# Two-block transformer kernel: the odd mixer's query/key units as 512-column products over two PSUM banks, and their move to the VectorE evacuation

## The chip, the cores and the metric

The kernel runs on one core of one Trainium2 chip. The metric is the device time of one execution in microseconds (us); before the change the median of three runs is 980.25 us (979.71 to 980.5).

## The reference, cut to what matters

Two transformer blocks run over 256 tokens of width 1024. The change lies in the second layer of the first block, the odd mixer (an mLSTM):

```python
p = (h @ w_in).astype(jnp.float32)          # h: 256 x 1024 (rmsnorm of x)
qk, v, og, ig_pre, fg_pre = jnp.split(p, splits, axis=-1)
qk = causal_conv_silu(qk, conv_w, conv_b)   # 4 taps along the tokens, 1024 channels
q, k = jnp.split(qk, 2, axis=-1)
...
ig = soft_cap(ig_pre + gb[0])               # 4 heads each
lf = jax.nn.log_sigmoid(soft_cap(fg_pre + gb[1]))
out = mlstm_scan(q, k, v, lf, ig)
```

## The kernel before, in words

**Products in two parts.** Every float32 weight w and activation h is split into a high and a low part (wh + wl, hh + hl). A projection is the sum of three products in the fp32r type: wh with hh, wh with hl, wl with hh. ScalarE (ACT) makes wh from the loaded weights (`high`, L1763), VectorE (DVE) makes wl by a subtraction (`split`, L1168: a helper for every tensor_tensor), both some three units ahead (AHEAD = 3) in rings of four slots (RING = 4).

**Units.** The weights are a list of 1 MB units (UNITS), taken in order by every engine's own loop `for u in range(NU)`. A unit of the kind F has 1024 rows by 256 columns: TensorE (PE) takes it as two groups g of 128 columns, each with 8 slabs k. A unit of the kind T has 512 rows by 512 columns, and two of them make one result. The order around the change is mv 0, mv 1, mqk 0 to 3, mv 2, mv 3, mog 0 to 3, then out2. The four mqk units are the query and key columns. hx holds hh and hl side by side, 256 tokens each.

**Two ways to do a unit of kind F.** `f_forward` puts both groups into one PSUM bank (2 x 256 columns) and issues, for each g and k, three products of 256 columns. `f_wide`, used for the units named in WIDE (attention and convolution of the second block), gives each group a bank of its own: 8 products of wh with the 512 columns of hh and hl together, then 8 products of wl with hh's 256 columns (`both_parts`). It needs a sum at the end: ACT copies columns 256 to 511 of each bank to the unit's home in SBUF (L2072) and counts S["wide"]; DVE then adds columns 0 to 255 to it (L1168, `tt(wide_home(u, g), wide_bank(u, g)[:, 0:SEQ], ...)`), twice a unit.

**The mqk units before.** They go through `f_forward`. ACT copies the bank of 2 x 256 columns to m_raw, a part of the arena (L2084). Between the products of mqk 0 lie 16 small products for the gates (`gate_product`, one after each slab's three).

**What DVE does there, in the order of its loop.** In the iteration of mqk 1: the gate sums gz (wait for PE's gmm), gz again after ACT's tanh (S["gcap"]), `split` of the unit three further on, and `conv_taps` of mqk 0 (one product with the row of rms values, then eight tap instructions). In the iteration of mqk 2: split, `conv_taps` of mqk 1. In mqk 3: gg and gB (from PE's gate_cumsum, counted S["g"]), split, `conv_taps` of mqk 2. In mv 2: a copy and a scan for the running maximum (S["M"], L1545, L1546), split, `conv_taps` of mqk 3. In mv 3: gm, eight instructions for m_w (S["warg"]), then `ml_probs` 0 and 1 (S["ms"]). All of this is one in-order queue.

**What PE does there.** After mqk 2: gate_cumsum; after mqk 3: gate_rows (wait for S["g"]); then mv 2; ml_scores 0 and 1; mv 3 with gate_max 0 and 1 among its first products (wait for S["M"]); ml_scores 2, which waits for `ml_probs(0)` because it takes the same bank (`eng.wait_ge(S["ms"], h - 1)`), and for S["qk"] at 4, ACT's silu of the last query/key pair; then mog 0.

Of the kernel before, what the change touches and what calls it, by code (L numbers as in the profile page):

```python
# [27 lines left out]
KT = D // P  # L28
# [126 lines left out]
def mlp(us, layer):  # L155
    for j in range(9):
# [12 lines left out]
NU = len(UNITS)  # L169
SLABS = {"F": KT, "C": KT, "T": 4, "B": 2}  # L170
EVAC = {"hf": "act", "hq": "act", "hi": "act", "rq": "dve", "rk": "dve", "rv": "act", "hgate": "act",
        "rgate": "act", "uw0": "act", "uw1": "act", "up0": "dve", "up1": "dve", "mqk": "act", "mv": "act", "mog": "act",
        "aq": "dve", "ak": "dve", "av": "act", "ag": "dve", "cc": "dve", "cx": "dve", "cb": "dve",
        "cg": "dve", "mc": "act", "ma": "act"}

# [4 lines left out]
_count, _in_bank, _next = {"act": 0, "dve": 0}, [None, None], 0  # L180


WIDE = ("aq", "ak", "ag", "cc", "cx", "cb", "cg")
WIDE_OF, PAIR_OF = {}, {}
for _u, (_kind, _, _, _, _role, _i) in enumerate(UNITS):
    if _role in WIDE:
        _n = WIDE_OF[_u] = len(WIDE_OF)
        PAIR_OF[_u] = ((3, 5), (2, 4), (0, 1))[_n % 3] if _n < 8 else ((3, 5), (0, 1))[_n % 2]
        if PAIR_OF[_u] == (0, 1):
            for _t in range(2):  # L190
                BEFORE[_u, _t] = _in_bank[_t]
                _in_bank[_t] = (_u, None)
        _count["dve"] += 1
        EVAC_AT[_u, None] = _count["dve"]
    elif _kind == "F":
        BANK_OF[_u] = _next
        BEFORE[_u, _next] = _in_bank[_next]
        _in_bank[_next] = (_u, None)
        _next ^= 1
        _count[EVAC[_role]] += 1  # L200
        EVAC_AT[_u, None] = _count[EVAC[_role]]
    elif _kind == "T":
        assert _next == 0
        T_OF[_u] = len(T_OF) // 2
        for _t in range(2):
            if _i % 2 == 0:
                BEFORE[_u, _t] = _in_bank[_t]
                _in_bank[_t] = (_u + 1, _t)
            else:
                _count[EVAC[_role]] += 1  # L210
                EVAC_AT[_u, _t] = _count[EVAC[_role]]
# [51 lines left out]
def build(nc, a, out):  # L263
    ctx = ExitStack()
    with ctx:
# [113 lines left out]
        m_raw = view(4096, 4, 2, SEQ)  # L379
# [183 lines left out]

        def wide_home(u, g):
            role, i = UNITS[u][4:]
            if role in ("aq", "ak", "ag"):
                return {"aq": a_q, "ak": a_k, "ag": a_g}[role][:, 2 * i + g, :]
            return (c_u if role == "cc" else c_t)[:, g * SEQ:(g + 1) * SEQ]
# [73 lines left out]
        def _(eng):  # L642
# [67 lines left out]
            def both_parts(o, u, g):  # L710

                c = slice(g * P, (g + 1) * P)
                for k in range(KT):
                    mm(o[:, :], slot(wh, u)[:, k, c], hx[:, k, :, :].rearrange("p a t -> p (a t)"), k == 0, False)
                for k in range(KT):
                    m = mm(o[:, 0:SEQ], slot(wl, u)[:, k, c], hh[:, k, :], False, k == KT - 1)
                return m

            def f_wide(u):

                n, w_hi, w_lo = WIDE_OF[u], slot(wh, u), slot(wl, u)
                if PAIR_OF[u] == (0, 1):
                    for t in range(TT):
                        wait_bank(eng, u, t)
                else:
                    for v in [v for v in WIDE_OF if v < u and PAIR_OF[v] == PAIR_OF[u]][-1:]:
                        wait_evac(eng, v)
                if u not in LOW_LAST:
                    for g in range(2):
                        m = both_parts(wide_bank(u, g), u, g)  # L730
                else:
                    for g in range(2):
                        for k in range(KT):
                            mm(wide_bank(u, g)[:, :], w_hi[:, k, g * P:(g + 1) * P], hx[:, k, :, :].rearrange("p a t -> p (a t)"), k == 0, False)
                    wait_low(eng, u)
                    for g in range(2):
                        for k in range(KT):
                            m = mm(wide_bank(u, g)[:, 0:SEQ], w_lo[:, k, g * P:(g + 1) * P], hh[:, k, :], False, k == KT - 1)
                m.then_inc(S["used"], 1)
# [16 lines left out]
            def f_forward(u):  # L756
                w_hi, w_lo, o = slot(wh, u), slot(wl, u), bank(u)
                wait_bank(eng, u, BANK_OF[u])
                for g in range(2):
                    for k in range(KT):  # L760
                        c, dst = slice(g * P, (g + 1) * P), o[:, g * SEQ:(g + 1) * SEQ]
                        mm(dst, w_hi[:, k, c], hh[:, k, :], k == 0, False)
                        mm(dst, w_hi[:, k, c], hl[:, k, :], False, False)
                        m = mm(dst, w_lo[:, k, c], hh[:, k, :], False, k == KT - 1)
                        if (g, k) == (1, KT - 1):
                            m.then_inc(S["used"], 1)
                        if u == at("mqk"):
                            gate_product(KT * g + k)

            def t_forward(u):  # L770

# [224 lines left out]
            def gate_max(j):  # L996

                if j == 0:
                    eng.wait_ge(S["M"], 1)
                for h in (2 * j, 2 * j + 1):  # L1000
                    mm(PS[5 + j][:, (h % 2) * SEQ:(h % 2 + 1) * SEQ],
                       ident[0:HEADS, h:h + 1].broadcast_to([HEADS, P]), MT, True, True)
                if j == 1:
                    for tt in range(TT):
                        m = eng.transpose(PS[7][:, 256 + 4 * tt:260 + 4 * tt], MT[:, tt * P:(tt + 1) * P],
                                          ident[0:HEADS, 0:HEADS])
                    m.then_inc(S["Mb"], 1)

            def ml_scores(h):
                eng.wait_ge(S["qk"], 2 if h < 2 else 4)  # L1010
                if h >= 2:
                    eng.wait_ge(S["ms"], h - 1)
                q, k, o = m_qk[:, h, :], m_qk[:, HEADS + h, :], PS[2 + h % 2]
                mm(o[:, 0:SEQ], k[:, 0:P], q, True, True)
                mm(o[:, SEQ:SEQ + P], k[:, P:2 * P], q[:, P:2 * P], True, True).then_inc(S["msc"], 1)
# [740 lines left out]
        def _(eng):  # L1756
# [246 lines left out]
            for u in range(-AHEAD, NU):  # L2003
# [42 lines left out]
                elif role in ("uw0", "uw1") and u in SECOND:  # L2046
                    for t in range(TT):
                        wait_evac(eng, u, t)
                        act(wf[:, half_of(t)], wf[:, half_of(t)], ACT.Square).then_inc(S["sq"], 1)
                elif UNITS[u][0] == "T" and i % 2 == 1 and u not in SECOND:  # L2050
                    for t in range(TT):
                        t_evac(u, t)
                elif role in ("rq", "rk"):
                    wait_used(eng, u)
                    j, swapped = rope_at(u)
                    if j >= 2:
                        eng.wait_ge(S["rope"], j - 1)
                    half = P // 2
                    for lo, hi in ((0, half), (half, 0)):
                        eng.copy(swapped[lo:lo + half], pair[hi:hi + half]).then_inc(S["swap"], 1)  # L2060
                elif role in WIDE:
                    if role == "cc" and i >= 1:
                        eng.wait_ge(S["c_gated"], i)
                    elif role == "cx":
                        eng.wait_ge(S["y_src"], i)
                    elif role == "cb":
                        eng.wait_ge(S["c_prod"], i + 1)
                    elif role == "cg":
                        eng.wait_ge(S["c_gated"], i + 1)
                    wait_used(eng, u)  # L2070
                    for g in range(2):
                        m = eng.copy(wide_home(u, g), wide_bank(u, g)[:, SEQ:2 * SEQ])  # L2072
                    m.then_inc(S["wide"], 1)
                elif role in ("up0", "up1"):
                    layer = 0 if role == "up0" else 1
                    c = slice(512 * (i % RING), 512 * (i % RING + 1))
                    wait_evac(eng, u)
                    act(wf[:, c], wf[:, c], ACT.Square).then_inc(S["sq"], 1)
                    eng.wait_ge(S["sq"], 16 * layer + i + 1)
                    if i >= RING:  # L2080
                        wait_used(eng, at(f"out{2 * layer + 1}", i - RING))
                    eng.copy(flat2(yh, i % RING), wf[:, c]).then_inc(S["yh"], 1)
                elif role == "mqk":
                    eng.copy(m_raw[:, i, :, :], pair).then_inc(S["evac_act"], 1)  # L2084

                if u == at("hf", 1):
                    eng.wait_ge(S["f"], 1)
# [77 lines left out]
```

## Time and profile before

| what | value |
|---|---|
| median of 3 runs | 980.25 us (979.71 to 980.5) |
| the profiled execution: time / span | 979.72 / 977.9 us |
| PE busy | 968.2 us, 99% |
| PE weight loads busy | 854.6 us, 87% |
| DVE busy | 661.6 us, 68% |
| ACT busy | 522.4 us, 53% |
| the mqk units on PE | 382.69 to 409.99 us |

Busy time of an engine is a mean over the span; a matmul's record is longer than the distance to the next one, since they are pipelined, so PE's pace is read from start to start.

### The profile page before, as it was taken

How to read it: one execution, taken by the hardware profiler on the slowest of the kernel's cores; microseconds unless marked ns; L12 is line 12 of the kernel's file. 1: busy time of each engine (PE TensorE's matmuls, PEld its weight loads, DVE VectorE, ACT ScalarE, POOL GpSimd, SP SyncE). 2: the span in 40 equal slices, each digit the busy share in tenths (PEclk: the TensorE clock that was granted, in tenths of full speed). 3: DMA queues.
4: the chain of work that ended last, by engine and by line, in shares of the span. 5: the costliest groups of instructions: out<-in, count | busy, mean ns of one | idle time of the engine just before them, and what ended most of it. 6: DMA issues, size and time to landing. Idle time of an engine off the chain costs nothing.

```text
span 977.9 us, 13743 instructions
## 1 busy us (share of the span) xinstructions
PE 968.2 (99%) x5616; PEld 854.6 (87%) x5616; DVE 661.6 (68%) x859; ACT 522.4 (53%) x671; POOL 13.9 (1%) x12
## 2 busy tenths in 40 slices
PE   9999999999999999999999999999999999999997
PEld 8898888899999988978899999987888888888885
DVE  6889646676666658766676666668655788756463
ACT  7744464654444447655664444448445576545533
POOL 0000000000000000000000000000000000002000
PEclk9999999999999999999999999999999999999999
DMA  9953526467777674534467777764865545566611
GB/s 328 300 173 129 172 92 196 137 213 250 243 237 226 227 238 133 186 129 129 151 215 225 260 229 232 247 183 145 271 205 178 170 134 170 172 213 222 210 44 44
DMA packets 122867, 187.32 MB, mean 192 GB/s; under 512 B 5332, under 2 KB 88757, under 8 KB 122805
## 3 DMA queue, kind: packets, MB, share of 16 engines
q1 hardware_dynamic: 122368, 186.05, 58.0%
q8 instruction: 45, 0.74, 0.3%
q10 hardware_dynamic: 436, 0.40, 0.1%
q14 instruction: 18, 0.14, 0.0%
HBM read 185.37 MB, written 1.06 MB: 191 GB/s over the span
## 4 chain that ended last, share of the span: by engine, by line
PE 93%; DVE 4%; ACT 1%; DMA 1%; issue 1%; DVEq 0%; ACTq 0%
PE bank L644 91%; DVE arena L1174 1%; DVE wl L1168 1%; DMA raw<-in_ev_w_in 1%; PE bank L878 1%; ACT wh L1763 1%; PE bank L968 0%; DVE arena L1171 0%; ACT arena L1758 0%; DVE arena L1168 0%; PE bank L1049 0%; ACT L1758 0%; PE bank L838 0%; PE bank L707 0%; DVE hx L1174 0%
## 5 line engine op out<-in xcount | busy, mean ns | idle before, releaser
L1168 DVE TENSOR_TENSOR wl<-raw,wh 128x2048 fp32r<-128x2048 f32 (+1 forms) x157 | 356.8, 2275 | 174.5 <-ACT wh L1763 101.1
L1763 ACT CAST wh<-raw 128x2048 fp32r<-128x2048 f32 x155 | 294.7, 1910 | 138.5 <-PE bank L644 134.8
L644 PE MATMUL bank<-hx,wh 128*128 128x256 f32 (+1 forms) x1728 | 346.1, 314 | 0.1
L644 PEld LDWEIGHTS bank<-hx,wh 128*128 128x128 f32 x1728 | 278.5, 191 | 15.9 <-issue 0.7
L644 PE MATMUL bank<-hx,wl 128*128 128x256 f32 x1088 | 238.6, 283 | 0.0
L644 PEld LDWEIGHTS bank<-hx,wl 128*128 128x128 f32 x1088 | 181.6, 191 | 4.4
L644 PE MATMUL bank<-wh,hx 128*128 128x512 f32 x576 | 184.4, 393 | 0.8 <-ACT arena L1758 0.5
L644 PE MATMUL bank<-wh,yh 128*128 128x512 f32 x416 | 162.7, 391 | 0.0
L644 PE MATMUL bank<-wl,yh 128*128 128x512 f32 x416 | 162.0, 390 | 0.0
L644 PE MATMUL bank<-wh,yl 128*128 128x512 f32 x416 | 161.9, 389 | 0.0
L644 PEld LDWEIGHTS bank<-wh,hx 128*128 128x128 f32 x576 | 107.9, 188 | 24.0 <-issue 1.9
L644 PE MATMUL bank<-wl,hx 128*128 128x512 f32 x288 | 112.2, 390 | 0.0
L644 PEld LDWEIGHTS bank<-wh,yl 128*128 128x128 f32 x416 | 78.1, 188 | 16.4
L644 PEld LDWEIGHTS bank<-wh,yh 128*128 128x128 f32 x416 | 78.2, 188 | 15.5
L644 PEld LDWEIGHTS bank<-wl,yh 128*128 128x128 f32 x416 | 78.2, 188 | 15.5
L1758 ACT ACTIVATE work<-work 128x512 f32<-128x512 f32 x32 | 20.0, 631 | 99.7 <-DVE work L1174 99.7
L1168 DVE TENSOR_TENSOR arena<-bank,arena 128x256 f32<-128x256 f32 (+1 forms) x88 | 40.6, 492 | 44.4 <-ACT arena L2072 28.0
L644 PEld LDWEIGHTS bank<-wl,hx 128*128 128x128 f32 x288 | 54.1, 188 | 10.7
L2072 ACT COPY arena<-bank 128x256 f32<-128x256 f32 x56 | 18.1, 376 | 72.5 <-PE bank L644 72.5
L1758 ACT ACTIVATE arena<-bank 128x512 f32<-128x512 f32 (+2 forms) x58 | 28.4, 498 | 35.0 <-PE bank L644 34.9
L1174 DVE SCALAR_TENSOR_TENSOR arena<-raw,cf,arena 128x256 f32<-128x256 f32 x84 | 40.7, 485 | 3.0
L1758 ACT ACT_TABLE_LOAD x26 | 33.4, 1283 | 4.3 <-PE bank L644 2.0
(184 smaller groups left out, 627.0 us busy)
## 6 DMA issues: line engine op xcount, KB each, us to landing
raw<-in_mlp_w SPq DMA_DIRECT2D x64, 1024.0 KB, 5.6
raw<-in_w_in SPq DMA_DIRECT2D x40, 1024.0 KB, 5.1
raw<-in_ev_w_in SPq DMA_DIRECT2D x19, 1024.0 KB, 5.2
raw<-in_w_ada SPq DMA_DIRECT2D x12, 1024.0 KB, 5.2
raw<-in_od_w_in SPq DMA_DIRECT2D x12, 1024.0 KB, 5.5
raw<-in_ev_w_out SPq DMA_DIRECT2D x6, 1024.0 KB, 4.8
raw<-in_od_w_out SPq DMA_DIRECT2D x4, 1024.0 KB, 4.9
raw<-in_w_o_conv SPq DMA_DIRECT2D x4, 1024.0 KB, 4.9
```

Source lines behind the costliest of these rows:

```text
L644: return eng.matmul(o, l, r, start=start, stop=stop, skip_group_check=True)
L878: m = eng.transpose(x_half(t, k), src[:, t, k * P:(k + 1) * P], ident[:, :])
L1168: return eng.tensor_tensor(o, x, y, op)
L1174: return eng.scalar_tensor_tensor(out=o, in0=x, scalar=c, in1=y, op0=op0, op1=op1)
L1758: return eng.activation(o, x, f, **more)
L1763: eng.copy(part(wh, u), part(raw, u)).then_inc(S["hi"], 1)
L2072: m = eng.copy(wide_home(u, g), wide_bank(u, g)[:, SEQ:2 * SEQ])
```

## The change

The units mqk 0 to 3 join WIDE and so go through `f_wide`, in the bank pairs (6, 7), (0, 1), (2, 3), (5, 6). Of the three products a slab, wh with hh and wh with hl become one of 512 columns. The home is m_raw. ACT's one copy of 512 columns a unit becomes two of 256, and DVE gets two additions of 128 x 256 a unit, at the place in its loop where f-units are evacuated: behind `conv_taps` of the unit before. The evacuation counts on DVE's semaphore. The gate products of mqk 0 stand behind the products of wl. Three waits are added on PE: mqk 2 and 3 wait for the evacuation of mqk 0, gate_max for that of the last unit in bank 6, ml_scores 0 and 1 for that of mqk 2. The second block's units keep their bank pairs.

```diff
-        "rgate": "act", ..., "mqk": "act", "mv": "act", "mog": "act",
+        "rgate": "act", ..., "mqk": "dve", "mv": "act", "mog": "act",
...
-WIDE = ("aq", "ak", "ag", "cc", "cx", "cb", "cg")
+WIDE = ("mqk", "aq", "ak", "ag", "cc", "cx", "cb", "cg")
...
-        PAIR_OF[_u] = ((3, 5), (2, 4), (0, 1))[_n % 3] if _n < 8 else ((3, 5), (0, 1))[_n % 2]
+        if _n < 4:
+            PAIR_OF[_u] = ((6, 7), (0, 1), (2, 3), (5, 6))[_n]
+        else:
+            PAIR_OF[_u] = ((3, 5), (2, 4), (0, 1))[(_n - 4) % 3] if _n < 12 else ((3, 5), (0, 1))[_n % 2]
...
+            if role == "mqk":
+                return m_raw[:, i, g, :]
...   in both_parts
                 for k in range(KT):
                     m = mm(o[:, 0:SEQ], slot(wl, u)[:, k, c], hh[:, k, :], False, k == KT - 1)
+                    if u == at("mqk"):
+                        gate_product(KT * g + k)
...   in f_wide
+                elif n in (2, 3):
+                    wait_evac(eng, at("mqk"))
...   in f_forward
-                        if u == at("mqk"):
-                            gate_product(KT * g + k)
...   in gate_max
                 if j == 0:
                     eng.wait_ge(S["M"], 1)
+                    wait_wide(eng, 6)
...   in ml_scores
                 if h >= 2:
                     eng.wait_ge(S["ms"], h - 1)
+                else:
+                    wait_evac(eng, at("mqk", 2))
...   on ScalarE
-                elif role == "mqk":
-                    eng.copy(m_raw[:, i, :, :], pair).then_inc(S["evac_act"], 1)
```

## Rows read from the trace of the kernel before

**Rows 1.** The page: busy time by engine, then TensorE's clock in 40 slices.

```profile
PE 968.2 (99%) x5616; PEld 854.6 (87%) x5616; DVE 661.6 (68%) x859; ACT 522.4 (53%) x671; POOL 13.9 (1%) x12
...
PEclk9999999999999999999999999999999999999999
```

**Rows 2.** Waits of PE in 365 to 470: releaser, us, times, longest.

```profile
PE bank L644 <- DVE arena L1174: 0.7, 1, 0.7
```

**Rows 3.** Busy time in stretches: mqk 0, mqk 2, one wide unit (us, then PE, PEld, ...).

```profile
382.69:391.97 9.28, 9.28 (x83) 9.28 (x82) 6.37 (x4) 4.12 (x3) 0.00 (x0) 1.00 0.70 227
...
397.81:403.57 5.76, 5.76 (x50) 5.76 (x49) 5.62 (x11) 2.59 (x3) 0.00 (x0) 1.00 0.55 185
...
688.18:693.77 5.59, 5.59 (x35) 4.92 (x33) 3.01 (x4) 3.88 (x4) 0.00 (x0) 1.00 1.10 349
```

**Rows 4.** Timeline of PE, wide unit (start, us, line, op, tiles, shape, count).

```profile
688.18 2.00 PE L644 MATMUL bank<-hx,wh 128*128 128x512 f32 x8
690.02 1.11 PE L644 MATMUL bank<-hx,wl 128*128 128x256 f32 x8
```

**Rows 5.** Timeline of ACT around the end of mqk 0.

```profile
392.03 0.58 ACT L2084 COPY arena<-bank 128x512 f32<-128x512 f32 x1 [5.22 <-PE bank L644]
392.51 1.90 ACT L1763 CAST wh<-raw 128x2048 fp32r<-128x2048 f32 x1
...
395.73 0.22 ACT L1758 ACTIVATE gcap<-gz 128x16 f32<-128x16 f32 x1
```

**Rows 6.** Timeline of DVE from mqk 0 to mv 3.

```profile
392.15 0.36 DVE L1174 SCALAR_TENSOR_TENSOR gz<-bank,rs,gzb 128x8 f32<-128x8 f32 x2 [2.10 <-PE bank L644]
395.98 0.17 DVE L1171 TENSOR_SCALAR gz<-gcap 128x16 f32<-128x16 f32 x1 [3.46 <-ACT gcap L1758]
...
408.79 0.16 DVE L1542 COPY gB<-bank 128x8 f32<-128x8 f32 x1
...
415.61 0.68 DVE L1546 TENSOR_TENSOR_SCAN work<-work 4x256 f32<-4x256 f32 x1
...
425.30 1.02 DVE L1174 SCALAR_TENSOR_TENSOR arena<-bank,arena 128x384 f32<-128x384 f32 x2
```

**Rows 7.** Timeline of PE: gate_rows, gate_max, mv 3's last product, ml_scores 2.

```profile
409.99 0.38 PE L993 MATMUL bank<-ident,gg 128*4 128x128 f32 x2
...
417.81 1.12 PE L644 MATMUL bank<-work,ident 4*128 4x256 f32 x4
...
424.87 0.39 PE L644 MATMUL bank<-wh,hx 128*128 128x512 f32 x1
426.00 1.55 PE L644 MATMUL bank<-arena 128*128 128x256 f32 x8 [0.74 <-DVE arena L1174]
```

**Rows 8.** Timeline of DVE, a wide unit's additions and the next instructions.

```profile
758.60 0.76 DVE L1168 TENSOR_TENSOR arena<-bank,arena 128x256 f32<-128x256 f32 x2 [1.43 <-ACT arena L2072]
759.27 0.61 DVE L1174 SCALAR_TENSOR_TENSOR work<-bank,bias 128x128 f32<-128x128 f32 x2
```

**Rows 9.** Groups of DVE's instructions in 684 to 800: busy, mean ns, idle before.

```profile
L1168 DVE TENSOR_TENSOR arena<-bank,arena 128x256 f32<-128x256 f32 x38 | 14.2, 418 | 21.2 <-ACT arena L2072 21.2
```

**Rows 10.** Timeline of ACT, a wide unit's copies and the next instruction.

```profile
691.17 0.65 ACT L2072 COPY arena<-bank 128x256 f32<-128x256 f32 x2 [1.57 <-PE bank L644]
691.71 1.93 ACT L1763 CAST wh<-raw 128x2048 fp32r<-128x2048 f32 x1
```

**Rows 11.** Busy time in stretches behind the last product (clock third from right).

```profile
971.24:973.00 1.76, 0.00 (x0) 0.00 (x0) 1.71 (x3) 0.29 (x1) 0.00 (x0) 1.00 0.00 0
...
974.00:975.00 1.00, 0.00 (x0) 0.00 (x0) 0.74 (x1) 0.72 (x1) 0.00 (x0) 1.00 0.00 0
975.00:975.50 0.50, 0.00 (x0) 0.00 (x0) 0.00 (x0) 0.00 (x0) 0.00 (x0) 0.55 0.00 0
```

**Rows 12.** DMA issues: the loads, seen in the queue's timeline and the page.

```profile
404.72 0.37 SPq L631 DMA_DIRECT2D raw<-in_od_w_in  x1
...
raw<-in_od_w_in SPq DMA_DIRECT2D x12, 1024.0 KB, 5.5
```

More of the change, by code:

```diff
@@ L171 @@
 EVAC = {"hf": "act", "hq": "act", "hi": "act", "rq": "dve", "rk": "dve", "rv": "act", "hgate": "act",
-        "rgate": "act", "uw0": "act", "uw1": "act", "up0": "dve", "up1": "dve", "mqk": "act", "mv": "act", "mog": "act",
+        "rgate": "act", "uw0": "act", "uw1": "act", "up0": "dve", "up1": "dve", "mqk": "dve", "mv": "act", "mog": "act",
         "aq": "dve", "ak": "dve", "av": "act", "ag": "dve", "cc": "dve", "cx": "dve", "cb": "dve",
```

## The prediction, made before the changed kernel was run

> **What bounds the kernel.** I read the page's busy times first: PE is busy for 968.2 of 977.9 us, at full clock in every slice [rows 1]. So the time is PE's work plus the few places where PE waits. The second view is therefore the list of PE's waits; around the change there is a single one, 0.7 us, for a DVE instruction at L1174 [rows 2]. The third is the timeline of the three engines from 382 to 432 us. The reader is to see two things in it. PE's units follow each other without a gap up to 425.26 us, and then PE stands until 426.00 [rows 7]. And DVE, which is busy 68% on the mean, has no idle time at all between 395.98 and the `ml_probs` at 425.30 for which PE waits: the only idle times noted are 2.10 us before the first gz and 3.46 us before the second [rows 6]. In this stretch DVE's queue is what ends last, and PE is the engine with slack.
>
> **PE's part of the change.** A narrow mqk unit takes 5.76 us (48 products of 256 columns, 0.12 us each), a wide unit 5.59 us [rows 3]: from the starts, 8 products of 512 columns take 1.84 us [rows 4], 0.230 each, which leaves 5.59 / 2 - 1.84 = 0.96 us for 8 of 256 columns. So a unit gives back 0.17 us. mqk 0 takes 9.28 us with its 16 gate products [rows 3], which is 3.52 us or 0.22 us each over a plain unit; each stands behind a product of wl both before and after, and goes back to a product of 256 columns in 14 cases of 16, so I keep 0.22. Four units: 4 x 0.17 = 0.68, taken as 0.7 us off PE's work. The Trainium skill, "TensorE: Matmul & The Clock Gate", section "Back-to-back issue gap", gives columns / 2.4 GHz + 2.5 ns; by that, one 512-column product in place of two of 256 saves only 2.5 ns, 0.16 us over the 64 pairs. The rows (0.230 against 0.240 us) give four times as much, and I go by them.
>
> **ACT's part.** One copy of 512 columns becomes two of 256. From the copy's start to the next instruction it was 0.48 us [rows 5]; for two copies it is 0.54 us [rows 10]: 0.06 us more. This counts once only. DVE's unbroken stretch starts when ACT's tanh is done (gcap, 395.73), and ACT reaches it by a chain (copy, cast, table load, tanh) from the copy of mqk 0 at 392.03, which waited for PE [rows 5]. PE ends mqk 0 0.18 us earlier (its 0.17, rounded with the gate products), the copies cost 0.06 more: DVE starts the stretch 0.12 us earlier. ACT's later copies are ready one DVE iteration before the additions that need them, so their 0.06 us are hidden behind DVE's own queue.
>
> **DVE's part.** Two additions of 128x256 are new in each unit, 8 in all. The trace has the very instruction in the second block: its record is 418 ns [rows 9], but consecutive ones overlap, and from the first of a pair to the instruction behind the pair is 759.27 - 758.60 = 0.67 us [rows 8]. DVE's own neighbours overlap in the same way in the stretch, and waits that are long met cost it nothing visible. The four pairs fall so:
>
> - mqk 0's pair comes at about 392.5, when ACT has copied, in the idle time before gcap. It pushes the first gz from 392.15 to about 393.3, and ACT reads gz only at 395.6. Hidden; without this cover it would be 0.67 us more.
> - mqk 1's, mqk 2's and mqk 3's pairs stand at the ends of their iterations, behind `conv_taps`, inside the stretch without idle time. Nothing hides them.
>
> So DVE is late by -0.12 + 0.67 = 0.55 us at the end of mqk 1's iteration, by 1.22 at gg and gB (408.79), and by -0.12 + 3 x 0.67 = 1.89 us at the scan (415.61) and at `ml_probs` (425.30) [rows 6]. Nothing is taken off DVE.
>
> **Who waits then.** At gate_rows PE would be 0.69 us early (409.30), but gB is done at 408.95 + 1.22 = 410.17: PE waits 0.9 us and is then 0.2 us late. At gate_max it would start at 418.0; the scan ends at 416.29 + 1.89 = 418.18: another 0.2. The last product of mv 3 ends at 425.26 + 0.4 = 425.7. ml_scores 2 started 0.13 us after `ml_probs(0)`; now that is 426.00 + 1.89 = 427.89. PE stands for 2.2 us instead of 0.74 [rows 7]. This last wait takes up the two before it and the whole of PE's saving. Behind PE's wait stand mog 0, ml_out and everything else, and from here to the end the other engines wait for PE (DVE ends its queue for the stage and waits for ml_out's sums), so the 1.89 us stay to the end.
>
> The other new waits are met long before. mqk 2 and 3 wait for mqk 0's pair, done at about 393.3 against 397.5. mv 2's bank is free after mqk 1's pair (about 403.5 against 410). ml_scores 0 needs mqk 2's pair, done at about 410.2 against 415.9. gate_max's wait for mqk 3's pair lies ahead of the scan on the same queue. On SP, the load issued at 404.72 waits for a split and goes out up to 1.2 us later; it lands 5.5 us later [rows 12], at about 411.5, and its unit (mog 3) is next touched by the cast behind ml_scores 2, after 426: hidden. ACT's silu of the last pair, its exponentials and its evacuation of mv 3 hang on `conv_taps` of mqk 3 and shift with DVE by the same 1.89, so they add nothing.
>
> **Sum.** The profiled execution took 979.72 us for a span of 977.9. Plus 1.89: span 979.8, time 981.6. The median of the runs is 0.53 us above this execution, so the median becomes 980.25 + 1.89 = 982.1 us, 0.19% slower. A measurement of this kernel tells about 0.2% (2.0 us) from no change; the forecast lies just within it.
>
> **Bounds.** The disputed price is the pair. Below: 0.67 us, from the pitch; a gain is excluded, as DVE loses no work. If the copies cost nothing more, 1.83 us. Above: the full records, 2 x 0.418 = 0.84 us. I take 0.67, the same instruction with another one directly behind it.
>
> **Rivals.**
>
> 1. *DVE pays full records* (slower beyond 0.2%). If each addition waited for the instruction before it to end, three pairs cost 2.51 - 0.12 = 2.39 us: 982.6 us, +0.24%. It decides from 0.693 us a pair on (3 x 0.693 - 0.12 = 1.96). For it: the additions read PSUM just filled, and stand between instructions that read SBUF alone, a neighbourhood of which rows 8 shows only one side. Against it: the 0.67. The Trainium skill, "VectorE: DVE Perf Modes", section on the TRN2 errata, has 120 + 256 cycles at 0.96 GHz for such an instruction, an estimate of 0.39 us each; by that the sum would be 3 x 0.78 - 0.12 = 2.2 us and 982.5. Chance 0.12.
> 2. *PE's saving is what remains* (not slower). If DVE's pairs were covered, the end would move by -0.7 us: 979.6, -0.07%. That needs 1.9 us of slack in DVE's stretch; rows 6 show none and rows 2 show PE already waiting for it. Chance 0.05.
> 3. *PE's clock falls in the longer wait* (slower). PE stands for 2.2 us. At the end of the kernel the granted clock is still 1.00 in the stretch from 974.00 to 975.00, with no product since 971.24, and falls to 1.2 GHz after 975.0 [rows 11]. A wait of 2.2 us is shorter. If it fell, the 24 products behind it (5.5 us) would take up to twice as long: up to 5.5 us more, 987. Chance 0.03.
>
> **Chances.** The forecast's mechanism gets 0.80. Its own spread is about 981.6 to 982.6; 980.25 plus 0.2% is 982.2, so it gives 0.46 to "within 0.2%", 0.31 to "slower" and 0.03 to "faster" (a scatter of 0.8 us between three runs, and effects I do not see). With the rivals: within 0.2% 0.46 + 0.05 = 0.51, slower 0.31 + 0.12 + 0.03 = 0.46, faster 0.03. The range, 981.1 to 983.1 us, goes from the forecast less the runs' scatter to rival 1 plus half of it.
>
> **What the changed profile would show.** Wide units of 5.6 us from about 391.8; mqk 0 of 9.1 us. On DVE, pairs of `arena<-bank,arena` at L1168 of 0.75 us, the first near 392.5 with idle time on both sides, the others with none. PE waits of about 0.9 us at gate_rows, 0.2 at gate_max and 2.2 at ml_scores 2, the last released by DVE at L1174 (stt). If ml_scores 2 starts before 427.5, the pairs were cheaper or covered; after 428.2, dearer. The prediction is wrong if the end moves by other than this start's shift, for then a wait further on has opened or closed.

## The result, and the profile after

The changed kernel takes 981.82 us (median of 17 runs, 981.47 to 983.7), the kernel before 979.95 us (17 runs, 979.59 to 981.16): 1.87 us more. The ratio of the runs is 1.002 with a 95% interval of 1.0012 to 1.0027. The forecast was 1.89 us more, 982.1 us from the median of the first three runs. At 0.19% the change lies, as forecast, just inside the 0.2% that the prediction took as its border. The profiled execution took 981.51 us against 979.72 us before, its span is 979.7 us against 977.9. One execution of e5 (3436 us) and one of e6 (1062 us) were far slower than all others of their kernel and are left out of the times and ratios below.

The page shows the trade in its first row: PE has 64 products fewer and 1.0 us less to do, DVE 8 instructions and 2.7 us more [rows 1].

```profile
PE 967.2 (99%) x5552; PEld 850.7 (87%) x5552; DVE 664.3 (68%) x867; ACT 522.5 (53%) x675; POOL 13.9 (1%) x12
```

PE's part, as busy time in stretches (us, then PE, PEld, DVE, ACT, POOL, the granted clock, DMA): mqk 0 and mqk 1 of the changed kernel.

```profile
382.57:391.71 9.14, 9.14 (x67) 8.45 (x66) 6.37 (x4) 4.13 (x3) 0.00 (x0) 1.00 0.72 227
391.71:397.38 5.67, 5.67 (x35) 4.99 (x34) 2.61 (x6) 5.32 (x7) 0.00 (x0) 1.00 0.51 193
```

mqk 0 takes 9.14 us, 0.14 less than before [rows 3]. mqk 2, from 397.38 to the gate_cumsum at 402.97, takes 5.59 against 5.76.

PE's waits between 365 and 470 us (releaser: us in total, times, longest):

```profile
PE bank L649 <- DVE arena L1184: 2.2, 1, 2.2
PE bank L1000 <- DVE gB L1552: 0.8, 1, 0.8
```

Before there was one, of 0.7 us [rows 2]. PE has done its part earlier and stands for longer, each time for DVE. DVE's timeline in the stretch (start, us, line, operation, tiles, shape, count, idle time ahead of it) shows the four pairs of additions; L1178 is the tensor_tensor helper now:

```profile
392.45 0.76 DVE L1178 TENSOR_TENSOR arena<-bank,arena 128x256 f32<-128x256 f32 x2 [2.51 <-ACT arena L2082]
393.12 0.35 DVE L1184 SCALAR_TENSOR_TENSOR gz<-bank,rs,gzb 128x8 f32<-128x8 f32 x2
395.79 0.17 DVE L1181 TENSOR_SCALAR gz<-gcap 128x16 f32<-128x16 f32 x1 [2.32 <-ACT gcap L1768]
...
402.23 0.75 DVE L1178 TENSOR_TENSOR arena<-bank,arena 128x256 f32<-128x256 f32 x2
402.89 2.28 DVE L1178 TENSOR_TENSOR wl<-raw,wh 128x2048 fp32r<-128x2048 f32 x1
...
409.20 0.75 DVE L1178 TENSOR_TENSOR arena<-bank,arena 128x256 f32<-128x256 f32 x2
409.87 0.15 DVE L1178 TENSOR_TENSOR gg<-gz,bank 128x8 f32<-128x8 f32 x1
...
416.32 0.74 DVE L1178 TENSOR_TENSOR arena<-bank,arena 128x256 f32<-128x256 f32 x2
416.99 0.40 DVE L1555 COPY work<-bank 4x256 f32<-4x256 f32 x1
417.42 0.68 DVE L1556 TENSOR_TENSOR_SCAN work<-work 4x256 f32<-4x256 f32 x1
...
427.12 1.02 DVE L1184 SCALAR_TENSOR_TENSOR arena<-bank,arena 128x384 f32<-128x384 f32 x2
```

The first pair has idle time ahead of it, and behind it only the two gz instructions before DVE stands idle again for 2.32 us: it costs nothing. The other three are followed at once by the next instruction, after 0.66, 0.67 and 0.67 us. `ml_probs` comes at 427.12 instead of 425.30 [rows 6], and ml_scores 2 on PE 0.70 us later, as before. PE's timeline, with the rows that answer to [rows 7]:

```profile
410.15 0.38 PE L1000 MATMUL bank<-ident,gg 128*4 128x128 f32 x2 [0.78 <-DVE gB L1552]
...
418.16 1.12 PE L649 MATMUL bank<-work,ident 4*128 4x256 f32 x4
...
427.82 1.55 PE L649 MATMUL bank<-arena 128*128 128x256 f32 x8 [2.19 <-DVE arena L1184]
```

ml_scores 2 starts at 427.82, 1.82 us later than before and between the forecast's limits of 427.5 and 428.2. The span grew by 1.8 us, so no wait further on opened or closed.

The part of the kernel ahead of mqk 0 differs between the profiled executions by up to 0.7 us (mqk 0 starts at 382.55 us in e8 and at 383.27 in e7). For the comparisons below I therefore use the **stage**: from the first product of mqk 0 to ml_scores 2. It is 426.00 - 382.69 = 43.31 us before and 427.82 - 382.57 = 45.25 us after: 1.94 us more.

### The profile page after: what moved, and what is told of

Its sections match the earlier page's. It is cut to its first block, busy times and chain, and to the rows that moved or that the text cites. A ratio compares the mean times of both kernels' runs of the same rounds, so it can differ in the third digit from the quotient of the medians.

```text
span 979.7 us, 13631 instructions
## 1 busy us (share of the span) xinstructions
PE 967.2 (99%) x5552; PEld 850.7 (87%) x5552; DVE 664.3 (68%) x867; ACT 522.5 (53%) x675; POOL 13.9 (1%) x12
## 4 chain that ended last, share of the span: by engine, by line
PE 92%; DVE 3%; ACT 2%; DMA 2%; issue 0%; ACTq 0%; DVEq 0%
PE bank L649 90%; DMA raw<-in_ev_w_in 1%; DVE arena L1184 1%; DVE wl L1178 1%; ACT wh L1773 1%; PE bank L885 1%; ACT arena L1768 1%; PE bank L975 0%; DMA x<-in_x 0%; DVE arena L1178 0%; DVE arena L1181 0%; PE bank L1059 0%; ACT L1768 0%; PE bank L845 0%; PE bank L712 0%
## 5 line engine op out<-in xcount | busy, mean ns | idle before, releaser
L1178 DVE TENSOR_TENSOR wl<-raw,wh 128x2048 fp32r<-128x2048 f32 (+1 forms) x157 | 356.7, 2275 | 172.8 <-ACT wh L1773 100.9
L649 PE MATMUL bank<-hx,wh 128*128 128x256 f32 (+1 forms) x1664 | 337.2, 319 | 0.1
L649 PEld LDWEIGHTS bank<-hx,wh 128*128 128x128 f32 x1664 | 270.2, 191 | 17.9 <-issue 0.7
L649 PE MATMUL bank<-hx,wl 128*128 128x256 f32 x1088 | 232.5, 284 | 0.0
L649 PEld LDWEIGHTS bank<-hx,wl 128*128 128x128 f32 x1088 | 179.0, 191 | 4.9
L1178 DVE TENSOR_TENSOR arena<-bank,arena 128x256 f32<-128x256 f32 (+1 forms) x96 | 43.6, 486 | 48.3 <-ACT arena L2082 32.0
L2082 ACT COPY arena<-bank 128x256 f32<-128x256 f32 x64 | 20.7, 376 | 85.9 <-PE bank L649 85.9
```

Of the source, the lines that this page charges most:

```text
L649: return eng.matmul(o, l, r, start=start, stop=stop, skip_group_check=True)
L1178: return eng.tensor_tensor(o, x, y, op)
```

## The experiments

The first three ask whether DVE's additions are the cause, or something on PE.

**e1: the kernel before plus DVE's additions alone.** Narrow units, old banks, old waits.

```diff
+                elif role == "mqk":
+                    wait_evac(eng, u)
+                    for g in range(2):
+                        tt(view(9216 + 512 * i + 256 * g, SEQ), PS[6][:, g * SEQ:(g + 1) * SEQ], x_row[2], ALU.add)
```

> The kernel before, with narrow units and its own banks and waits, and two DVE additions of 128x256 (one operand from PSUM) put in behind conv_taps in each mqk iteration, their result unused. Theory A (the additions in DVE's unbroken stretch are the cause): three pairs at 0.67 us lie in the stretch, so the end moves by 3 x 0.67 = 2.0 us, 0.20%, and PE's wait at ml_scores 2 grows from 0.74 to about 2.7 us. Theory B (the cause is on PE: the new waits for evacuations, or the bank pairs): none of these is in this kernel, so no change.

Measured: 981.86 us, ratio 1.0021 (1.0013 to 1.003). The stage is 428.32 - 383.01 = 45.31 us, 2.00 more than before. PE's waits in it:

```profile
PE bank L644 <- DVE arena L1174: 2.2, 1, 2.2
PE bank L993 <- DVE gB L1542: 0.2, 1, 0.2
```

This is theory A's number, without any of PE's edits; theory B falls. The wait at ml_scores 2 is 2.2 us and not 2.7, since 0.54 us of the lateness had been met before it: gate_max starts 35.66 us after the stage's start, before it was 35.12 [rows 3, 7]. The length of the last wait is not the delay; the stage is.

**e2: the changed kernel with additions of 8 columns.**

```diff
-                        m = tt(wide_home(u, g), wide_bank(u, g)[:, 0:SEQ], wide_home(u, g), ALU.add)
+                        n = 8 if role == "mqk" else SEQ
+                        m = tt(wide_home(u, g)[:, 0:n], wide_bank(u, g)[:, 0:n], wide_home(u, g)[:, 0:n], ALU.add)
```

> The changed kernel with the additions of the mqk units cut from 256 to 8 columns each; it leaves out the sum of the high and low parts for the other 248 columns. Theory A: a pair costs about 0.14 us in place of 0.67, so the stretch ends 1.6 us earlier than in the changed kernel: 0.3 us over the kernel before, and not 0.7 under it, since DVE still ends last and PE's saving goes into the wait. Theory B: all of PE's new waits, banks and products are still there, so the time stays 1.9 us over the kernel before.

Measured: 980.29 us, ratio 1.0002 (0.9994 to 1.0011), 0.24 us over the 980.05 of the kernel before beside it. The stage is 426.61 - 382.94 = 43.67 us. With all of PE's products, banks and waits of the change, and nearly no additions, 1.6 us of the 1.94 are gone. And the time is not under that of before: `ml_probs` comes 425.90 - 382.94 = 42.96 us after the stage's start, 42.61 before, so DVE alone forbids a gain, whatever PE saves. The rows for `ml_probs` and for PE's wait for it:

```profile
425.90 1.02 DVE L1184 SCALAR_TENSOR_TENSOR arena<-bank,arena 128x384 f32<-128x384 f32 x2
...
426.61 1.55 PE L649 MATMUL bank<-arena 128*128 128x256 f32 x8 [0.17 <-DVE arena L1184]
```

**e5: the additions twice.** The changed kernel, each mqk pair issued first into an unused place of the arena.

```diff
+                    if role == "mqk":
+                        for g in range(2):
+                            tt(view(9216 + 256 * g, SEQ), wide_bank(u, g)[:, 0:SEQ], wide_home(u, g), ALU.add)
```

> The changed kernel with each mqk pair of additions issued twice, the first time into an unused place. Theory A: three more pairs in the stretch, 3 x 0.67 = 2.0 us more: 3.9 us over the kernel before, 0.4%, with PE's wait at ml_scores 2 at about 4.2 us. If PE's clock falls in a wait of that length, the granted clock behind it shows 1.2 GHz and the time is several us more. Theory B: no change against the changed kernel.

Measured: 983.63 us (median of three runs, 983.63 to 984.5), ratio 1.0039 (1.0024 to 1.0054); the stage is 429.91 - 382.68 = 47.23 us, 3.92 over before. The size is as expected, the place of the waits is not:

```profile
PE bank L1000 <- DVE gB L1552: 2.1, 1, 2.1
PE bank L649 <- DVE work L1556: 0.8, 1, 0.8
PE bank L649 <- DVE arena L1184: 0.6, 1, 0.6
```

Most of the lateness is now met at gate_rows and gate_max, and TensorE's clock took part: it fell to 1.2 GHz behind gate_max, from about 423.3 to 426.7 us, so that PE, although the stretch was longer, waited only 0.6 us at ml_scores 2.

```profile
420.00:422.00 2.00, 1.75 (x7) 1.15 (x7) 2.00 (x2) 0.00 (x0) 0.00 (x0) 1.00 0.00 0
422.00:424.00 2.00, 2.00 (x10) 1.52 (x9) 1.93 (x5) 0.00 (x0) 0.00 (x0) 0.83 0.41 37
424.00:426.00 2.00, 2.00 (x6) 1.57 (x5) 1.93 (x5) 0.00 (x0) 0.00 (x0) 0.50 0.85 338
426.00:428.00 2.00, 2.00 (x9) 1.59 (x8) 2.00 (x8) 1.45 (x2) 0.00 (x0) 0.82 0.37 150
```

(Busy time in stretches; the third number from the right is the granted clock.) PE still waits for `ml_probs` at ml_scores 2, so this fall costs nothing here.

The next three ask whether DVE's queue can be emptied in other ways, and what PE's saving is worth then.

**e3: the changed kernel, two weight splits of DVE moved.** The split of mv 2 goes ahead of the wait for the tanh, into the idle time after gz; the split of mog 1 goes behind `ml_probs` 0 and 1.

```diff
+                    split(at("mv", 2))
                     eng.wait_ge(S["gcap"], 1)
...
+                if u == at("mv", 3):
+                    split(at("mog", 1))
                 for s in splits_at(u)[u in GROUP_AT:]:
...
-                    if split_by(s) == "dve":
+                    if split_by(s) == "dve" and s not in (at("mv", 2), at("mog", 1)):
```

> The changed kernel with two weight splits of DVE moved: the one of mv 2 goes ahead of the wait for the tanh, into idle time (stretch 1.5 us earlier), and the one of mog 1 goes behind ml_probs 0 and 1 (2.2 us less ahead of PE's wait). Theory A: DVE is early by 3.7 us, more than the waits at gate_rows, gate_max and ml_scores 2, so all three vanish: PE keeps its 0.7 us and gets the 0.74 us that the kernel before waited: 1.4 us under the kernel before, 978.5. Theory B (new waits on PE for evacuations cost time themselves): less than that, by what they cost.

Measured: 978.27 us, ratio 0.9984 (0.9975 to 0.9993). PE waits for nobody between 365 and 470 us, and the stage is 424.48 - 382.74 = 41.74 us, 1.57 under before. `ml_probs` 0 is in time now:

```profile
394.49 2.29 DVE L1178 TENSOR_TENSOR wl<-raw,wh 128x2048 fp32r<-128x2048 f32 x1 [0.85 <-issue]
...
423.57 1.02 DVE L1184 SCALAR_TENSOR_TENSOR arena<-bank,arena 128x384 f32<-128x384 f32 x2
424.51 4.48 DVE L1178 TENSOR_TENSOR wl<-raw,wh 128x2048 fp32r<-128x2048 f32 x2
```

The waits that the change adds on PE cost nothing that can be seen, so no part is left to theory B. Two of the eleven runs lie higher, at 979.84 and 979.85 (see e9).

**e4: the kernel before, the same two splits moved.**

> The kernel before with the same two splits moved. Theory A: only the wait of 0.74 us at ml_scores 2 vanishes: 979.2, 0.08% under the kernel before; against e3 the difference is PE's own gain from the wide units, 0.7 us. A rival (the moved splits are late for other work): a new wait on PE at mog 1 or in the loads, no gain.

Measured: the median is 980.53 us, ratio 0.9998 (0.9989 to 1.0007): by the median a miss of 1.3 us. But the eleven runs form two groups, 978.73 to 979.06 (five) and 980.53 to 980.69 (six), and the mean granted clock goes with them: 0.998 to 0.999 in the lower, 0.996 to 0.997 in the upper. The profiled execution is of the lower group; its stage is 425.40 - 383.00 = 42.40 us, 0.91 under before, with no wait in it. Expected were 0.74 us, the wait as the view lists it. That counts from the end of a record of 0.39 us. But in e4, without the wait, ml_scores 2 starts 0.22 us behind the start of the last product of mv 3; before, that would have been at about 425.1 and not 425.26, so the wait cost 0.9 us [rows 7]. Against e3's 41.74 PE's own gain from the wide units is 0.66 us, the forecast's 0.69. The rows of e4:

```profile
425.18 0.39 PE L644 MATMUL bank<-wh,hx 128*128 128x512 f32 x1
425.40 1.47 PE L644 MATMUL bank<-arena 128*128 128x256 f32 x8
```

The upper group is the subject of e8.

**e6: the changed kernel, only the split of mog 1 moved.**

> The changed kernel with only the split of mog 1 moved behind ml_probs 0 and 1. Theory A: ml_probs 0 is done 2.2 us earlier, but gB is as late as in the changed kernel, so the wait of 0.8 us at gate_rows stays and eats PE's saving: the wait at ml_scores 2 is about 0, and the time about 0.2 us under the kernel before (979.8). If PE's saving came through whole, it would be 1.4 us.

Measured: 979.73 us as the median, ratio 1.0002 (0.9992 to 1.0011), unclear by itself. The runs form groups here too: six from 979.21 to 979.73 us with a clock of 0.998 or 0.999, three from 980.61 to 980.78 with 0.996, one at 982.73 with 0.995. In the profiled execution, of the first group, the stage is 425.95 - 382.92 = 43.03 us, 0.28 under before. The wait at ml_scores 2 is gone, the one at gate_rows stays:

```profile
PE bank L1000 <- DVE gB L1552: 0.8, 1, 0.8
```

ml_scores 2 starts 0.70 us after `ml_probs` (425.25), the same distance as where PE waits, so DVE is still just last. The other 1.29 us that e3 has over this kernel come with the first move, which brings gB, the scan and `ml_probs` forward together.

**e7: GpSimd takes the product with the rms row.** The changed kernel, relieving DVE in another way.

```diff
-                wait_evac(eng, u)
-                link(tt(ps, ps, x_rms(2), ALU.mult))
+                eng.wait_ge(S["rms"], i + 1)
...   on GpSimd
+                if role == "mqk":
+                    wait_evac(eng, u)
+                    eng.tensor_tensor(m_raw[:, i, :, :], m_raw[:, i, :, :], x_rms(2), ALU.mult).then_inc(S["rms"], 1)
```

> The changed kernel with the product of m_raw and the row of rms values (128x512, four times) moved from DVE to GpSimd. Theory A: DVE's stretch loses four steps of 0.72 us, 2.9 us, so all of PE's waits there vanish: 1.4 us under the kernel before, 978.5, as in e3. A rival: GpSimd takes 1.7 us for such an instruction and may slow DVE or come late for conv_taps (it has 2.1 us of split ahead of each); then DVE's instructions beside it are longer or DVE waits, and less is gained.

Measured: 983.52 us, ratio 1.0036 (1.0024 to 1.0049), worse than the changed kernel. What theory A led me to expect failed here; the rival named with it came true. GpSimd's timeline:

```profile
393.99 1.30 POOL L2137 TENSOR_TENSOR arena<-arena,tables 128x512 f32<-128x512 f32 x1 [393.54 <-DVE arena L1178]
403.01 3.29 POOL L2137 TENSOR_TENSOR arena<-arena,tables 128x512 f32<-128x512 f32 x1 [7.73 <-DVE arena L1178]
410.56 3.41 POOL L2137 TENSOR_TENSOR arena<-arena,tables 128x512 f32<-128x512 f32 x1 [4.26 <-DVE arena L1178]
418.22 1.27 POOL L2137 TENSOR_TENSOR arena<-arena,tables 128x512 f32<-128x512 f32 x1 [4.25 <-DVE arena L1178]
```

and DVE's:

```profile
402.85 2.28 DVE L1178 TENSOR_TENSOR wl<-raw,wh 128x2048 fp32r<-128x2048 f32 x1
406.33 0.74 DVE L1181 TENSOR_SCALAR arena<-arena,col 128x256 f32<-128x256 f32 x2 [1.20 <-POOL arena L2137]
...
418.49 1.54 DVE L1555 TENSOR_TENSOR_SCAN work<-work 4x256 f32<-4x256 f32 x1
```

The product takes 1.3 us while DVE is mostly idle or runs small instructions, and 3.3 to 3.4 us when DVE's split of 2.28 us runs beside it. DVE then waits 1.2 us, twice; its scan beside GpSimd's last product takes 1.54 us instead of 0.68. The steps saved are lost again: `ml_probs` comes 45.04 us after the stage's start, 44.55 in the changed kernel. And PE's clock was at 1.2 GHz from about 421.0 to 427.8 us, so that PE, not DVE, was last at ml_scores 2:

```profile
428.31 1.02 DVE L1184 SCALAR_TENSOR_TENSOR arena<-bank,arena 128x384 f32<-128x384 f32 x2
...
430.48 1.47 PE L649 MATMUL bank<-arena 128*128 128x256 f32 x8
```

By DVE alone it would have started 0.70 us after `ml_probs`, at 429.01. So of the 1.96 us that e7's stage is longer than the changed kernel's, 0.49 are DVE's and 1.47 come with the slow clock.

I had priced the product by 1.7 us, the mean of GpSimd's eight products of this size in the profile before, and not by what runs beside it. That trace held two prices, not one: six of the eight took 1.29 to 1.31 us, and two, each beside a split of DVE, 2.93 and 2.95. Two of its rows:

```profile
866.87 1.29 POOL L2122 TENSOR_TENSOR yl<-arena,yh 128x512 fp32r<-128x512 f32 x1 [22.02 <-ACT yh L1857]
884.99 2.93 POOL L2122 TENSOR_TENSOR yl<-arena,yh 128x512 fp32r<-128x512 f32 x1 [16.83 <-ACT yh L1857]
```

**e8 and e9: gate_max over 128 rows.** The falls of the clock in e2 and e5 come behind gate_max, whose products have 4 rows (`bank<-work,ident 4*128 4x256`), and the fall in e7 at the end of the first four of its eight products. These two kernels are e4 and e3 with the same products over all 128 rows, 124 of them weighted with zero.

```diff
-                       ident[0:HEADS, h:h + 1].broadcast_to([HEADS, P]), MT, True, True)
+                       ident[:, h:h + 1].broadcast_to([P, P]), wf[:, SEQ:2 * SEQ], True, True)
```

> The kernel of e4 (before, two splits moved), whose runs fell into two groups, 978.7 to 979.1 and 980.5 to 980.7 us, the upper one with a mean granted clock of 0.996 to 0.997 against 0.998 to 0.999. The eight products of gate_max here use all 128 rows of the array instead of 4 (124 of them weighted with zero; the same result and the same columns). Theory C: TensorE's clock falls in some executions behind gate_max, as the profiles of e2, e5 and e7 show from 420 to 428 us, because these products use 4 rows; then with 128 rows all runs lie at 978.9 with a clock of 0.998 to 0.999. A rival: the fall comes from something else there (waits of PE, the float32 form); then the two groups stay.

> The changed kernel with the two splits moved (e3) and the same eight products over 128 rows. Theory C: the two of eleven runs of e3 at 979.8 vanish, and all lie at 978.2 (0.18% under the kernel before). A rival: nothing changes against e3, and some runs stay at 979.8.

Measured, e8: 978.41 us, ratio 0.998 (0.9971 to 0.9989); all eleven runs lie between 978.11 and 978.59 with a clock of 0.998 or 0.999. The upper group is gone: six of eleven runs in e4, none of eleven here. e4 was measured earlier and on another chip, but of the 20 runs of the kernel before beside e8 seven have a mean clock of 0.996, so the falls had not gone by themselves. e9: 978.07 us, ratio 0.9978 (0.9969 to 0.9988), ten runs from 977.85 to 978.59, with none like e3's two at 979.84 and 979.85; after two of eleven, ten without one can be chance. e9 has the lowest median of all and beats both kernels; against e8, whose median is 0.34 us higher, I have no interval.

Three things stay open. The traces kept of e4 and e8 are both without a fall, so it is inferred, not seen, that e4's upper group falls behind gate_max. In its favour: the falls in e2 and e5 last 3.4 us, which at half the clock is an estimate of 1.7 us lost, and the two groups of e4 lie 1.7 us apart. Next, the products over 128 rows are also done sooner, so whether the rows or the time decides is not separated. Last, the mean clock is a rough sign, for e2's profiled run has 0.998 in spite of its fall.

There was a gain that I had not expected: the products cost less in place. The starts of the two groups of gate_max in e3, and then in e9, with three wide products of mv 3 between them:

```profile
417.19 1.12 PE L649 MATMUL bank<-work,ident 4*128 4x256 f32 x4
...
419.14 1.12 PE L649 MATMUL bank<-work,ident 4*128 4x256 f32 x4
```
```profile
417.18 1.03 PE L649 MATMUL bank<-work,ident 128*128 128x256 f32 x4
...
418.74 1.02 PE L649 MATMUL bank<-work,ident 128*128 128x256 f32 x4
```

1.56 us in place of 1.95, for the same columns. e8's stage is 424.54 - 382.55 = 41.99 us, 0.41 under e4's. In e9 PE reaches ml_scores 2 early enough to meet `ml_probs` again, and the stage is 424.37 - 382.82 = 41.55 us, 0.19 under e3's.

## Why the prediction was right

The stage in each kernel, its difference from the kernel before, and what was expected of the whole:

| kernel | stage, us | against before | expected |
|---|---|---|---|
| before | 43.31 | | |
| changed | 45.25 | +1.94 | +1.89 |
| e1, additions alone | 45.31 | +2.00 | +2.0 |
| e2, additions of 8 columns | 43.67 | +0.36 | +0.3 |
| e5, additions twice | 47.23 | +3.92 | +3.9 |
| e4, before, splits moved | 42.40 | -0.91 | -0.74 |
| e3, changed, splits moved | 41.74 | -1.57 | -1.4 |
| e6, one split moved | 43.03 | -0.28 | -0.2 |
| e7, GpSimd | 47.21 | +3.90 | -1.4 |
| e8, as e4, 128 rows | 41.99 | -1.32 | -1.1 (978.9) |
| e9, as e3, 128 rows | 41.55 | -1.76 | -1.8 (978.2) |

- **PE's gain.** Forecast 0.7 us. Units of 5.59 against 5.76, and e4 against e3 gives 0.66. Right, and lost in the changed kernel, as e1 shows: with the additions but narrow units the stage is only 0.06 longer.
- **The price of a pair.** Forecast 0.67 us; measured 0.66, 0.67, 0.67, so rival 1 falls. The Trainium skill, "VectorE: DVE Perf Modes", section on the TRN2 errata, has 120 + 256 cycles at 0.96 GHz for such an instruction, an estimate of 0.39 us for one addition and 0.78 for a pair. This trace, with 0.66 to 0.67 us in a row of instructions without waits, does not agree.
- **Cover.** mqk 0's pair was hidden, the three others were not. Right.
- **The start of DVE's stretch.** Forecast 0.12 us earlier; counted from the stage's start, the second gz came at 395.79 - 382.57 = 13.22 us against 395.98 - 382.69 = 13.29: 0.07 earlier. mqk 0 saved 0.14 us and not 0.18. This small miss is the 0.05 us between 1.89 and 1.94.
- **Waits.** Forecast were 0.9 us at gate_rows, 0.2 at gate_max and 2.2 at ml_scores 2. Measured were 0.8 and 2.2; at gate_max none is listed, but it starts 0.53 us after the start of the product ahead of it, against 0.33 before, which is the 0.2.
- **Rival 2** (PE's saving remains) falls with the wait of 2.2 us. It needed slack in DVE's queue; e3 makes that slack, and there it is true.
- **Rival 3** was half right in a way that I had not thought of. I asked whether a wait of 2.2 us lets the clock fall. In the profile of the changed kernel it stood at 1.00 through the wait:

```profile
426.00:427.80 1.80, 0.00 (x0) 0.01 (x1) 1.76 (x6) 1.79 (x6) 0.00 (x0) 1.00 0.00 0
```

  But the clock does fall in some executions at another place, behind gate_max, and to judge by the mean clock in the kernel before too: of the 33 runs of it beside e1 to e4 the ten with a mean clock of 0.996 lie at 980.25 to 980.69, the fastest at 979.55 with 0.999. There the fall costs less than in e4, plausibly because part of it passes in the wait of 0.74 us that follows; in the changed kernel, where that wait is 2.2 us, runs of 981.53 us have clocks of 0.997 as well as 0.999. That the wait covers the fall is argued from these numbers, not shown by a run made for it. The runs at 983.3 and 983.7 of the changed kernel are not explained; e1, with narrow units, has such runs too (983.48 and 983.67), so they need none of PE's edits.

## What to carry to other kernels

An engine that is 68% busy on the mean can be the one that ends last in a stage: look for its stretch without idle time, and count what an edit adds inside it and what before it, separately. Time an added instruction by the distance to its follower in the trace, not by its record. Where the saving is on the engine that waits, first move work of the other engine out of the stretch (two splits moved gave 0.9 us of the stage in the kernel before and 3.5 us in the changed one, and nothing of it was lost later in the profiled executions); only then is a cheaper form of product worth anything. And where a group of instructions has one mean, look at its single records before you price by it: two prices can be mixed in it.

## What the runs showed of the hardware

- TensorE's granted clock fell to 1.2 GHz for 3.4 us in the profiles of e2 (from about 420.8) and e5 (from about 423.3), both times behind the eight products of 4 rows (gate_max), and for 6.8 us in that of e7, from 421.0 on, at the end of the first four. In the order of e4 six of eleven runs were 1.7 us slower with the lower mean clock; with 128 rows none of eleven was.
- In e2 no wait of PE stood near the fall. Busy time in stretches around and behind gate_max (417.4 to 420.5 us), the granted clock third from the right:

```profile
418.00:420.00 2.00, 2.00 (x9) 1.20 (x8) 1.96 (x3) 0.00 (x0) 0.00 (x0) 1.00 0.00 0
420.00:421.00 1.00, 1.00 (x7) 0.82 (x6) 0.96 (x4) 0.00 (x0) 0.00 (x0) 0.89 0.77 106
421.00:422.00 1.00, 1.00 (x3) 0.79 (x3) 0.96 (x3) 0.00 (x0) 0.00 (x0) 0.50 1.02 410
```

  Here PE's records fill every stretch and the clock fell, while in the changed kernel's profile it stood at 1.00 through a wait of 2.2 us with nothing on PE.
- Four products with 4 rows and the three behind them took 1.95 us (e3); with 128 rows 1.56 us (e9).
- A two-input instruction of GpSimd on SBUF (128x512) took 1.3 us alone and 3.3 to 3.4 us beside DVE's two-input split, which itself kept its 2.28 us. Of the 3.29 us of the second one, 1.17 lie behind the end of the split at 405.13, so beside the split it got hardly forward (an estimate from these rows: alone it takes 1.3). DVE's scan, however, went from 0.68 to 1.54 us beside GpSimd's product.
